# Scattering expert results to token rows and loading them in order, in a one-core block kernel

## The reference

```python
g_sel = jnp.argmax(g_logits, axis=-1)                   # one of 4 groups
e_logits = take_along_axis(e_logits, g_sel)              # the 4 experts of that group
top_p, top_i = lax.top_k(e_prob, TOP_K_IN_GROUP)         # 2 of them
weights = p_g * top_p / sum(top_p)
expert_id = g_sel[:, None] * EXPERTS_PER_GROUP + top_i   # 16 experts in all
for e in range(N_EXPERTS):
    h = jax.nn.silu(xt @ w_gate[e]) * (xt @ w_up[e])     # hidden width 256
    y = y + combine[:, e:e + 1] * (h @ w_down[e])
```

## Time and profile before

| | us |
|---|---|
| median of 3 runs | 2644.7 |
| lowest and highest run | 2642.81, 2647.73 |
| profiled execution, its own time | 2642.54 |
| span of the profiled execution | 2640.7 |
| mixture: first gather issued, first feed-forward product | 234.60, 442.94 |

### The profile page before, as it was taken

How to read it: one execution, slowest core, us unless ns; L and a number is a source line. 1 busy time by engine, 2 the same in 40 slices (tenths; PEclk the granted TensorE clock), 3 DMA queues, 4 the chain that set the end, 5 groups by cost and what they waited for, 6 DMA issues and landing times. The chain is left out here.

```text
span 2640.7 us, 31200 instructions
## 1 busy us (share of the span) xinstructions
PE 2556.0 (97%) x12661; PEld 2063.1 (78%) x12661; DVE 1312.9 (50%) x1708; ACT 930.7 (35%) x1262; POOL 201.1 (8%) x162
## 2 busy tenths in 40 slices
PE   7997996999999999999999999999999999999998
PEld 7876775788888878778888888888887777888886
DVE  5456996534345443654343454444543446544444
ACT  4344883322233234542222332222412255322222
POOL 0002112400003300100000000000050001000000
PEclk9998998999999999999999999999999999999999
DMA  4116994222224321223222232222332213232222
GB/s 147 57 56 234 408 387 149 92 96 96 96 82 132 102 72 54 76 88 96 92 93 95 88 104 96 93 98 89 119 108 87 66 35 102 88 100 92 96 94 74
DMA packets 88869, 292.37 MB, mean 111 GB/s; under 512 B 11522, under 2 KB 16530, under 8 KB 88466
## 3 DMA queue, kind: packets, MB, share of 16 engines
q1 hardware_dynamic: 81634, 264.10, 30.0%
q0 software_dynamic: 6224, 23.60, 2.3%
q10 hardware_dynamic: 864, 2.62, 0.2%
HBM read 276.12 MB, written 12.58 MB: 109 GB/s over the span
## 5 line engine op out<-in xcount | busy, mean ns | idle before, releaser
L496 PE MATMUL bank_l<-xg_hi,w_hi 128*128 128x512 f32 (+1 forms) x2144 | 841.4, 392 | 16.1 <-DVE w_lo L462 16.1
L496 PE MATMUL bank_l<-xg_lo,w_hi 128*128 128x512 f32 (+1 forms) x2144 | 838.8, 391 | 0.0
L496 PE MATMUL bank_l<-xg_hi,w_lo 128*128 128x512 f32 (+1 forms) x2144 | 834.4, 389 | 0.0
L462 DVE TENSOR_TENSOR w_lo<-w_raw,w_hi 128x1024 fp32r<-128x1024 f32 (+2 forms) x424 | 506.3, 1194 | 301.6 <-ACT w_hi L457 300.2
L457 ACT ACTIVATE w_hi<-w_raw 128x1024 fp32r<-128x1024 f32 (+2 forms) x424 | 427.6, 1010 | 445.4 <-PE bank_l L496 424.9
L496 PEld LDWEIGHTS bank_l<-xg_hi,w_hi 128*128 128x128 f32 x2144 | 403.6, 188 | 113.8 <-DVE w_lo L462 15.3
L496 PEld LDWEIGHTS bank_l<-xg_lo,w_hi 128*128 128x128 f32 x2144 | 402.9, 188 | 90.4 <-issue 2.2
L496 PEld LDWEIGHTS bank_l<-xg_hi,w_lo 128*128 128x128 f32 x2144 | 404.1, 188 | 87.5
L496 PE MATMUL bank_l<-hid_hi_ff,w_lo 128*128 128x512 f32 x704 | 280.9, 399 | 0.0
L496 PE MATMUL bank_l<-hid_lo_ff,w_hi 128*128 128x512 f32 x704 | 277.4, 394 | 0.0
L496 PE MATMUL bank_l<-hid_hi_ff,w_hi 128*128 128x512 f32 x704 | 276.0, 392 | 0.0
(11 more groups left out here) (386 smaller groups left out, 2531.9 us busy)
## 6 DMA issues: line engine op xcount, KB each, us to landing
w_raw<-in_ff_gate SPq DMA_DIRECT2D x88, 512.0 KB, 3.4
w_raw<-in_ff_up SPq DMA_DIRECT2D x88, 512.0 KB, 3.5
expert_raw<-in_experts SPq DMA_DIRECT2D x81, 512.0 KB, 19.2
w_raw<-in_in SPq DMA_DIRECT2D x80, 512.0 KB, 3.4
w_raw<-in_ff_down SPq DMA_DIRECT2D x64, 512.0 KB, 3.4
w_raw<-in_out SPq DMA_DIRECT2D x24, 512.0 KB, 3.5
w_raw<-in_ff_down SPq DMA_DIRECT2D x32, 384.0 KB, 3.0
w_raw<-in_experts SPq DMA_DIRECT2D x15, 512.0 KB, 20.1
```

Of the source, the lines that this page charges most:

```text
L462: dve.tensor_tensor(lo, panel_memory(i), hi.bitcast(F32), ALU.subtract).then_inc(*panel_lo.done(i))
L496: done = pe.matmul(dst, w[:, c * cols:(c + 1) * cols], moving, start=c == 0 and n == 0, stop=c == kc - 1 and n == 2)
```

## The change

Every pair gets a row number instead of a slot: choice k of token t is row k x 512 + t. The constant `token_id` becomes `row_id`, the row number less 1,024, so that the product of the one-hot matrices is the row number less 1,024 where a place is filled and 0 where it is empty. VectorE adds 1,024 (`row_f`), takes 512 off where the number is 512 or more (`second`), and casts to `token_of` and `row_of`. For an empty place `token_of` is 512 and `row_of` is 1,024, both past the last row. Gathers and stores get a bounds check that skips such rows: an empty place of `x_slot` keeps what was in it. The stores of `y_slot` become indirect scatters to `y_rows`, which now has 1,024 rows in the order of pairs; the last tile's is one of them, issued by GpSimd. At the end SyncE loads `y_pair` from `y_rows` with eight plain transfers, behind `main_tiles_done` in its own queue and in front of its other panels; `slot_of` and the eight gathers of GpSimd are gone.

```diff
-                    token_id = sb(routing, "token_id", [P, TB])
+                    row_id = sb(routing, "row_id", [P, TOP_K * TB])
...
-        y_rows = nc.dram_tensor("y_rows", (TILES * P, D), F32, kind="Internal").ap()
+        y_rows = nc.dram_tensor("y_rows", (TOP_K * T, D), F32, kind="Internal").ap()
...
-            dve.tensor_copy(token_of[:, :], bank_s[:, 0, 0:TILES]).then_inc(*step("token_of"))
-            dve.tensor_copy(slot_of[:, :, :], slot_f[:, :, :, :].rearrange("p k b o -> p (b o) k")).then_inc(
-                *step("slot_of"))
+            dve.tensor_scalar(row_f[:, :], bank_s[:, 0, 0:TILES], float(TOP_K * T), None, ALU.add).then_inc(*step())
+            follows()
+            dve.tensor_scalar(second[:, :], row_f[:, :], float(T), -float(T), ALU.is_ge, ALU.mult).then_inc(*step())
+            follows()
+            dve.tensor_tensor(token_of[:, :], row_f[:, :], second[:, :], ALU.add).then_inc(*step("token_of"))
+            dve.tensor_copy(row_of[:, :], row_f[:, :]).then_inc(*step("row_of"))
...
-            at, y = (run.first_tile + run.n - 1) * P, m["y_slot"][:, (run.n - 1) % 2, :]
-            act.wait_ge(*run.y_low.upto(run.n - 1))
-            act.dma_start(y_rows[at:at + P, 0:512], y[:, 0:512]).then_inc(*run.stored_last.done(0))
-            act.wait_ge(*run.y_high.upto(run.n - 1))
-            act.dma_start(y_rows[at:at + P, 512:], y[:, 512:]).then_inc(*run.stored_last.done(1))
...
                     out=m["x_slot"][:, i % 2, :], out_offset=None, in_=x_rows,
-                    in_offset=bass.IndirectOffsetOnAxis(ap=token_of[:, at:at + 1], axis=0)
+                    in_offset=bass.IndirectOffsetOnAxis(ap=token_of[:, at:at + 1], axis=0),
+                    bounds_check=T - 1, oob_is_err=False
...
-                if 0 < i < run.n:
+                if i:
                     pool.wait_ge(*run.y_low.upto(i - 1))
                     pool.wait_ge(*run.y_high.upto(i - 1))
-                    at = (run.first_tile + i - 1) * P
-                    pool.dma_start(y_rows[at:at + P, :], m["y_slot"][:, (i - 1) % 2, :]).then_inc(
-                        *run.stored[(i - 1) % 2].done(i - 1))
+                    at = run.first_tile + i - 1
+                    pool.indirect_dma_start(
+                        out=y_rows, out_offset=bass.IndirectOffsetOnAxis(ap=row_of[:, at:at + 1], axis=0),
+                        in_=m["y_slot"][:, (i - 1) % 2, :], in_offset=None,
+                        bounds_check=TOP_K * T - 1, oob_is_err=False
+                    ).then_inc(*run.stored[(i - 1) % 2].done(i - 1))
...
-            def fetch_rows(source):
-                for blk in range(TB):
-                    for i in range(TOP_K):
-                        to = pool.indirect_dma_start(
-                            out=y_pair[:, blk, i, :], out_offset=None, in_=source,
-                            in_offset=bass.IndirectOffsetOnAxis(ap=slot_of[:, blk, i:i + 1], axis=0))
...
+            main_tiles_done(sp)
+            for blk in range(TB):
+                for i in range(TOP_K):
+                    at = i * T + blk * P
+                    sp.dma_start(y_pair[:, blk, i, :], y_rows[at:at + P, :]).then_inc(*y_fetched[blk].done(i))
```

More of the change, by code:

```diff
@@ L264, in build @@
         with ExitStack() as phase:
-            slot_of = sb(phase, "slot_of", [P, TB, TOP_K], U32)
             token_of = sb(phase, "token_of", [P, TILES], U32)
+            row_of = sb(phase, "row_of", [P, TILES], U32)
             weight = sb(phase, "weight", [P, TOP_K, TB, 1])
@@ L293, in build @@
                     slot_f = sb(routing, "slot_f", [P, TOP_K, TB, 1])
-                    token_id = sb(routing, "token_id", [P, TB])
+                    row_id = sb(routing, "row_id", [P, TOP_K * TB])
+                    row_f = sb(routing, "row_f", [P, TILES])
+                    second = sb(routing, "second_choice", [P, TILES])
                     bounds = sb(routing, "bounds", [P, 1, TILES + 1])
@@ L1206, in routing_dve @@
             dve.wait_ge(loaded["columns"], 16)
-            dve.wait_ge(loaded["token_id"], 16)
+            dve.wait_ge(loaded["row_id"], 16)
             for k in range(pairs):
                 dve.tensor_scalar(slot_hot[:, k, :], columns[:, :], in_tile[:, k, :],
-                                  token_id[:, k % TB:k % TB + 1], ALU.is_equal, ALU.mult).then_inc(
+                                  row_id[:, k:k + 1], ALU.is_equal, ALU.mult).then_inc(
                     *shaped.done(("slot_hot", k)))
             dve.wait_ge(*mixed.upto("token_of"))
-            dve.tensor_copy(token_of[:, :], bank_s[:, 0, 0:TILES]).then_inc(*step("token_of"))
-            dve.tensor_copy(slot_of[:, :, :], slot_f[:, :, :, :].rearrange("p k b o -> p (b o) k")).then_inc(
-                *step("slot_of"))
+            dve.tensor_scalar(row_f[:, :], bank_s[:, 0, 0:TILES], float(TOP_K * T), None, ALU.add).then_inc(*step())
[4 more added lines that the diff above has]
+            dve.tensor_copy(row_of[:, :], row_f[:, :]).then_inc(*step("row_of"))
             follows()
@@ L1263, in __init__ @@
                 self.stored = [steps(f"{tag}_stored{i}", 16) for i in range(2)]
-                self.stored_last = steps(f"{tag}_stored_last", 16)
         def tiles_pe(pe, run, panel_ready, panel_tiles, panel_used):
@@ L1484, in main_tiles_done @@
             e.wait_ge(*tile_run.y_low.upto(N_EXPERTS - 1))
-            e.wait_ge(*tile_run.stored[(N_EXPERTS - 3) % 2].upto(N_EXPERTS - 3))
             e.wait_ge(*tile_run.stored[(N_EXPERTS - 2) % 2].upto(N_EXPERTS - 2))
-            e.wait_ge(*tile_run.stored_last.upto(1))
+            e.wait_ge(*tile_run.stored[(N_EXPERTS - 1) % 2].upto(N_EXPERTS - 1))
         def over_tiles_done(e):
@@ L1491, in over_tiles_done @@
             e.wait_ge(*over_run.y_low.upto(OVERFLOW - 1))
-            e.wait_ge(*over_run.stored[(OVERFLOW - 3) % 2].upto(OVERFLOW - 3))
             e.wait_ge(*over_run.stored[(OVERFLOW - 2) % 2].upto(OVERFLOW - 2))
-            e.wait_ge(*over_run.stored_last.upto(1))
+            e.wait_ge(*over_run.stored[(OVERFLOW - 1) % 2].upto(OVERFLOW - 1))
         def mixture_pe(pe):
@@ L1522, in mixture_act @@
             act.wait_ge(rows_written, 16 * TB)
-            act.wait_ge(*routed.upto("slot_of"))
+            act.wait_ge(*routed.upto("row_of"))
             tiles_act(act, tile_run, lambda e, i, j: round_ahead(e, ("experts", (i, j))), used)
@@ L1579, in mixture_pool @@
             routing_pool(pool)
-            pool.wait_ge(*routed.upto("slot_of"))
+            pool.wait_ge(*routed.upto("row_of"))
             pool.wait_ge(rows_written, 16 * TB)
             tiles_pool(pool, tile_run)
-            def fetch_rows(source):
-                for blk in range(TB):
-                    for i in range(TOP_K):
-                        to = pool.indirect_dma_start(
-                            out=y_pair[:, blk, i, :], out_offset=None, in_=source,
-                            in_offset=bass.IndirectOffsetOnAxis(ap=slot_of[:, blk, i:i + 1], axis=0))
-                        to.then_inc(y_fetched[blk].handle, 16)
-                        y_fetched[blk].values[i] = 16 * (i + 1)
             with pool.If(tiles_over(pool) > 0):
@@ L1596, in mixture_pool @@
                 over_tiles_done(pool)
[L1597 to L1600, removed]
         def mixture_sp(sp):
@@ L1611, in mixture_sp @@
                     load(sp, "columns", columns[:, :], dram["columns"])
-                    load(sp, "token_id", token_id[:, :], dram["token_id"])
+                    load(sp, "row_id", row_id[:, :], dram["row_id"])
                     load(sp, "numbers", numbers[:, :, :], dram["numbers"])
@@ L2550, in constants @@
         "masks": masks, "far_masks": far_masks, "resets": resets, "gla_mask": gla_mask,
-        "token_id": (np.arange(TB)[None, :] * P + i[:, None]).astype(np.float32),
+        "row_id": (np.arange(TOP_K * TB)[None, :] * P + i[:, None] - TOP_K * T).astype(np.float32),
         "columns": np.broadcast_to(i[None, :].astype(np.float32), (P, P)).copy(),
```

## The result

| | us |
|---|---|
| changed kernel, median of 10 runs | 2652.27 (2649.09 to 2655.22) |
| kernel before, 10 runs beside it | 2646.45 (2641.62 to 2647.77) |
| ratio | 1.0024, 95% interval 1.0016 to 1.0031 |
| span of the profiled execution | 2648.2 |

The change costs 5.8 us by the medians, 4.2 to 8.2 by the interval: slower, by 0.22% in the middle, with the 0.2% that was set as the bound of "same" inside the interval.

What follows compares the result with a forecast made beforehand. TensorE, busy 97% of the span, was taken as the bound, so time moves only where it stands still. End of the mixture +3.5, late gather -1.3, first gather -0.5 give +1.7 us on 2644.7: 2646.4 us, range 2640 to 2654.

Steps and rivals of the forecast that it cites:

- the forecast itself: Whole kernel: the summed case, 2646.4 us, with its own range of 2643 to 2650; chance 0.45.
- the likeliest class: Whole kernel: time the same within 0.2% (5.3 us), 2639.4 to 2650.0 us; chance 0.67.
- rival 3: End of the mixture: the last scatter lands slowly, in 8.9 us, moving all behind it by 5.4 us: 2651.8; chance 0.15.
- the tail: End of the mixture: products start 5.4 us sooner, then stand still for a late panel; net cost 3.5 us.
- The stall: Products of y_pair: the panel behind eight loads delays VectorE's additions; TensorE stands still 6.4 us and its clock falls.
- The gain in the loop: Tile loop: skipping empty rows shortens transfers, so the one late gather (tile 4) is in time: gain 1.3 us.
- The first gather: Start of the mixture: the first gather, not behind a store, lands sooner with half its rows: gain 0.5 us.
- Rival 2: Tile loop: skipping brings nothing and the gather is late as before: 2648.2 us; chance 0.25.
- Rival 4: Tile loop: the bounds check makes scatter and gather issue take 2 us each, 20 us in all: some 2666; chance 0.07.
- Rival 5: End of the mixture: the panel, ninth load, isn't late, so the 5.4 us are a gain: 2637.5 us; chance 0.08.

Runs made afterwards that it cites:

- a: Changed kernel with SyncE's load of the third feed-forward panel moved in front of main_tiles_done: 2642.78 us, ratio to the kernel before 0.9992.
- b: Changed kernel with the load of the third feed-forward panel behind four of the eight y_pair loads: 2643.32 us, ratio to the kernel before 0.9995.
- g: Changed kernel with main_tiles_done and the eight y_pair loads in GpSimd's program instead of SyncE's: 2644.05 us, ratio to the kernel before 0.9996.
- j: Changed kernel with the third feed-forward panel's load behind main_tiles_done, in front of all eight y_pair loads: 2643.87 us, ratio to the kernel before 0.9996.
- i_before_copy: Kernel before the change, but for the last tile both engines copy their half before splitting the first feed-forward panel: 2645.51 us, ratio 1.0000.
- c: Run a, but gathers skip nothing: token numbers of empty places cut to 511, no bounds check on gathers: 2642.99 us, ratio to the kernel before 0.9993.
- h: Run a, but scatters skip nothing: empty places go to spare rows of y_rows, no bounds check on scatters: 2645.13 us, ratio to the kernel before 1.0000.
- e: Run a, plus both engines copy the last tile's half before splitting the first feed-forward panel: 2639.42 us, ratio to the kernel before 0.9976.
- f: Run e, plus the first block's y_pair rows loaded as four 256 KB transfers, first two with their own semaphore: 2641.96 us, ratio to before 0.9986.
- d_after_again: The changed kernel unaltered, timed once more: 2652.43 us, ratio to the kernel before 1.0024.
- e_again: The kernel of run e unaltered, timed once more on another chip: 2641.00 us, ratio to the kernel before 0.9979.
- f_again: The kernel of run f unaltered, timed once more on another chip: 2639.34 us, ratio to the kernel before 0.9974.

## Why the prediction was right or wrong

The time, 2652.3, lies in the range of 2640 to 2654, but outside the 2643 to 2650 of the forecast itself, and the likeliest class, within 0.2%, was missed by a hair. The change was put at +1.7 us and measured +5.8. That the wide range holds the time is partly luck: the nearest figure of the prediction is rival 3's 2651.8, and its mechanism is wrong. The path was right; two terms of the sum were not, the gains of 1.3 and 0.5 us, which no run shows, and the tail was put too small.

- *The stall* was right in place and form: the panel behind the eight loads, VectorE's additions behind its split, one gap after two half blocks, and the clock at 0.50 behind it. The runs a, b, g and j show it.
- *Its size* was too small. The tail was put at +3.5 us and is +4.83, or +5.27 (38.62 against the 33.35 of i_before_copy). Up to the first load the steps nearly hold: 0.84 us to wake GpSimd instead of 0.54, and 3.45 to land instead of 3.5. Behind it, the first product came 5.66 us after the first load instead of 4.9, and the panel 15.1 us instead of 14.2; each load in front of the panel took 1.46 us ((15.11 - 3.4) / 8) instead of 1.35. The gap is 6.80 us (6.4), the six half blocks behind it 13.38 (13.15).
- *The gain in the loop*, 1.3 us, is the step that failed. It was to come from fewer rows in the queue. The late gather wasn't cured in this trace: 0.76 of the 1.29 us are left, the landing fell by 0.4 us in the median, and 0.7 of longer issue of the scatter and 0.2 of the gather stood against it. In other traces this wait is gone and short ones at other tiles have come, and c, which gathers every row, is no worse. The loop is shorter by 0.44 us, less than two executions of one kernel differ by.
- *The first gather*, 0.5 us, can't be told: from the logits to the first transposes it is 25.1 to 28.4 us in the traces, in kernels with skipping, without it and before the change alike.
- *Rival 2* (skipping brings nothing) was thus nearer than the forecast. It had 2648.2, a change of +3.5; with the tail as measured that would be +4.8. Of the distance to 2652.3 that is left, 1.75 us are the kernel before itself, whose median is 2646.45 over ten runs and was 2644.7 over three; 1.0 us is then still open, and the stretch *rest*, below, is 0.7 longer.
- *Rival 3* is wrong: SyncE's first load follows the last scatter's issue by 3.45 and 3.98 us. *Rival 4* is wrong as well: the scatter takes 1.30 us, not 2, and the 0.9 us a tile that scatter and gather take longer were hidden. The check isn't what makes the scatter long: without it, in h, it takes 1.39 us in the median. The gathers take 1.12 us without it (c), 1.17 with it and 0.97 in the kernel before, so most of their longer issue isn't the check either. *Rival 5* is wrong for the changed kernel. The run a takes the lateness away and nothing else; it is 0.08% under the kernel before, not the 7.2 us (0.27%) of that rival, and only e and f, with further edits, come to 0.14 to 0.26%.
- *Rest*: 0.2 to 0.8 us more in the runs with the new scatter (2198.00 to 2198.57; d_after_again 2199.68, 1.9 more) than in both traces without it (2197.76). It was not foreseen and its cause is open.

## What to carry to other kernels

A transfer moved to another engine's queue stands in front of everything that this queue issues later; look up what is next in it, who waits for that, and who stands behind the waiting instruction. Here eight loads that came 4 us sooner made a panel late, and the traces show the additions held up behind that panel's split. Writing the additions ahead of the split would be another cure; it wasn't tried. Leaving out half of the rows of the gathers brought nothing that a run shows.

## What the runs showed of the hardware

- An indirect scatter with separate rows takes 3.3 to 4.7 us from its issue to the transfer that waits for it, where no panel loads run beside it, and 7.6 with panel loads beside it (one trace). The landing itself reads 3.2 to 3.9 us in the traces that have it and skip rows (a, d, e_again, f_again); a plain store of 512 KB into idle engines took 2.9.
- GpSimd takes 1.30 us in the median to issue an indirect scatter, 1.17 an indirect gather with a bounds check, 1.12 one without (c), and 0.57 a plain store of 512 KB.
- Skipping half of the rows of a 128-row gather leaves its median time to land among full queues as it was: 8.4 to 8.6 against 8.6 us.
- The granted clock dips below 1.00 while TensorE is busy, 0.83 at 30 to 40 in the profile before with 9.97 of 10 us busy, and not at the same places in each execution. The same code reaches one point at 214.2 to 218.1 us, and nine or more runs of one kernel on one chip spread by 5 to 12 us. Stretches of a trace tell more than medians about where a few us went, but they vary by 1 to 2 us as well.
